# A two-block transformer kernel on one core: bias tile from 16 row copies, stacked narrow projections, last chunk by token tile, and the order of the splits

## The reference, cut to what matters

```python
# block 1
proj = rmsnorm(x) @ w_in            # qa, ka, va, qb, kb, vb, g_low (16 wide), ob, gate_a, gate_b
ya   = sliding_window_attention(qa, ka, va)  # 16 heads; score + bias[head, query - key], softmax
log_a = log_sigmoid(g_low @ w_gate_up + b_gate) / 16
ob   = gated_linear_attention(qb, kb, vb, log_a)   # 4 heads, chunks of 64 tokens
h    = x + (sigmoid(gate_a) * (ya @ w_proj_a) + sigmoid(gate_b) * (norm(ob) * silu(..) @ w_proj_b)) @ w_out
h    = h + (silu(z @ w_ffn_gate) * (z @ w_ffn_up)) @ w_ffn_down
# block 2 (input: rmsnorm(h)): memory attention over 256 memory rows, a causal convolution,
# latent attention: queries from c_q (512 wide), keys/values from c_kv (512), and one rope key
# k_rope_raw (64 wide) shared by 16 heads, rotated with cos/sin of the positions
out  = x2 + merged @ w_o            # last product of the kernel, 2048 x 2048
```

## Time and profile before

| | |
|---|---|
| median of 3 runs | 2601.61 us |
| the profiled execution's own time | 2602.74 us |
| its span | 2600.9 us |
| PE busy (matmul) | 2557.3 us, 98% |
| DVE busy | 1538.7 us, 59% |
| ACT busy | 1131.9 us, 44% |
| mean granted clock of PE | 0.995 |
| mean DMA rate | 180 GB/s |

### The profile page before, as it was taken

One profiled execution on the slowest core, in us unless ns is written; L12 is line 12 of the kernel. 1 busy time (PEld: TensorE's weight loads), 2 busy tenths in 40 slices (PEclk: granted clock), 3 DMA queues, 4 the chain that ended last, 5 costly groups with the idle time before them and its releaser, 6 DMA issues.

```text
span 2600.9 us, 30707 instructions
## 1 busy us (share of the span) xinstructions
PE 2557.3 (98%) x11746; PEld 2103.1 (81%) x11746; DVE 1538.7 (59%) x2102; ACT 1131.9 (44%) x1435; POOL 0.2 (0%) x4
## 2 busy tenths in 40 slices
PE   8899999999999999999999999999999999999999
PEld 7688777888778888888888888788888888888887
DVE  5566565466555655556556664557557757564554
ACT  4344334444444444433455454433434545444443
POOL 0000000000000000000000000000000000000000
PEclk9999999999999999999999999999999999999999
DMA  8845446655666566665656565555665455456654
GB/s 235 250 147 151 126 146 197 194 183 185 194 187 181 180 190 193 186 191 181 199 193 205 175 192 166 166 178 167 190 189 167 154 158 167 145 185 175 194 189 131
DMA packets 236404, 466.94 MB, mean 180 GB/s; under 512 B 19131, under 2 KB 27745, under 8 KB 235889
## 3 DMA queue, kind: packets, MB, share of 16 engines
q1 hardware_dynamic: 230688, 455.23, 56.4%
q10 hardware_dynamic: 5584, 9.94, 1.7%
HBM read 459.87 MB, written 5.24 MB: 179 GB/s over the span
## 4 chain that ended last, share of the span: by engine, by line
PE 90%; DVE 5%; DMA 2%; ACT 2%; issue 1%; ACTq 0%; DVEq 0%
PE acc L470 25%; PE acc L472 25%; PE acc L471 25%; PE banks L608 3%; DVE w_lo L1525 2%; PE banks L829 2%; PE banks L828 2%; PE banks L830 2%; PE acc L828 1%; PE acc L830 1%; PE acc L829 1%; DMA raw<-in_w_in_dram 1%; ACT w_hi L1119 1%; DMA arena<-bias_rows 1%; PE banks L979 1%
## 5 line engine op out<-in xcount | busy, mean ns | idle before, releaser
L1525 DVE TENSOR_TENSOR w_lo<-raw,w_hi 128x1024 fp32r<-128x1024 f32 (+1 forms) x866 | 1042.1, 1219 | 891.1 <-ACT w_hi L1119 860.4
L1119 ACT ACTIVATE w_hi<-raw 128x1024 fp32r<-128x1024 f32 (+1 forms) x866 | 904.3, 1054 | 1128.0 <-PE acc L472 1004.2
L470 PE MATMUL acc<-w_hi,x_hi_A 128*128 128x512 f32 x1880 | 746.9, 397 | 5.1 <-DVE w_lo L1525 5.1
L472 PE MATMUL acc<-w_hi,x_lo_A 128*128 128x512 f32 x1880 | 734.5, 391 | 0.0
L471 PE MATMUL acc<-w_lo,x_hi_A 128*128 128x512 f32 x1880 | 733.7, 390 | 0.0
L470 PE MATMUL acc<-w_hi,x_hi_B 128*128 128x512 f32 (+1 forms) x1216 | 474.8, 390 | 8.5 <-DVE w_lo L1525 8.5
L472 PE MATMUL acc<-w_hi,x_lo_B 128*128 128x512 f32 (+1 forms) x1216 | 471.2, 387 | 0.0
L471 PE MATMUL acc<-w_lo,x_hi_B 128*128 128x512 f32 (+1 forms) x1216 | 470.9, 387 | 0.0
L470 PEld LDWEIGHTS acc<-w_hi,x_hi_A 128*128 128x128 f32 x1880 | 354.3, 188 | 87.8 <-issue 10.2
L472 PEld LDWEIGHTS acc<-w_hi,x_lo_A 128*128 128x128 f32 x1880 | 353.9, 188 | 75.5
L471 PEld LDWEIGHTS acc<-w_lo,x_hi_A 128*128 128x128 f32 x1880 | 354.6, 189 | 71.1 <-issue 0.5
(11 more groups left out here) (263 smaller groups left out, 1336.4 us busy)
## 6 DMA issues: line engine op xcount, KB each, us to landing
raw<-in_w_in_dram SPq DMA_DIRECT2D x377, 512.0 KB, 4.4
raw<-in_w_ffn_gate_dram SPq DMA_DIRECT2D x88, 512.0 KB, 4.1
raw<-in_w_ffn_up_dram SPq DMA_DIRECT2D x88, 512.0 KB, 4.3
raw<-in_w_ffn_down_dram SPq DMA_DIRECT2D x88, 512.0 KB, 4.6
raw<-in_w_out_dram SPq DMA_DIRECT2D x32, 512.0 KB, 4.5
raw<-in_w_mem_kv_dram SPq DMA_DIRECT2D x32, 512.0 KB, 4.7
raw<-in_w_mla_out_dram SPq DMA_DIRECT2D x32, 512.0 KB, 4.7
raw<-in_w_o_dram SPq DMA_DIRECT2D x32, 512.0 KB, 4.7
```

The lines of the kernel that those rows point to most:

```text
L470: mm(o, xh, hi[:, k, :], start=(kt == first_k), stop=False)
L472: last = mm(o, xl, hi[:, k, :], start=False, stop=(kt == (last_k or c.kts) - 1))
L1119: act.activation(w_hi[:, s, 0:n], raw[:, r, 0:n], ACT.Copy).then_inc(hi_done, 1)
L1525: dve.tensor_tensor(w_lo[:, s, 0:n], raw[:, r, 0:n], w_hi32[:, s, 0:n], ALU.subtract).then_inc(lo_done, 1)
```

## The change

Seven edits go together.

1. The bias rows are written 16 times per head instead of 128 (`BCOPY`), from ScalarE's queue. The tile is read back in 8 DMAs of 16 partitions from SP's queue, after the loads of chunk `kva`, behind a wait for the write. VectorE makes the bias row ahead of the row statistics instead of in the middle of the first chunk's evacuation.
2. VectorE no longer waits for the Sin.
3. `glow` and `kr` are done with high and low weights side by side as one stationary operand (`stacked`): 32 matmuls each. `glow` leaves 32 rows, summed by a `w_gate_up` loaded twice. `kr` becomes two granules of eight k-tiles after an undivided `cq`, leaves 128 rows, and is turned and summed by two small matmuls with a folded identity before granule 4 of `ckv`.
4. The last chunk of `w_o` runs four granules as before, waits for all four others, and then does these for token tile 0 and after it for token tile 1; each tile is added and stored by itself.
5. TensorE transposes quarter 1 of `x` after granule 0, and 2 and 3 after granules 2 and 4; the split counts become 3, 2, 2, 1.
6. ScalarE does both `back(3)` of a head ahead of the Square.
7. ScalarE runs one tiny Copy before anything else, after a VectorE memset.

```diff
+BCOPY = 16
+STACKED = ("glow", "kr")
-    out += [("cq", 1, [Chunk("cq", "A", 0, CQ_HEAD, 2, CW, "w_in_2", C2["cq"])])]
-    out += [one("kr", "A", 0, KT, "w_in_2", C2["kr"], w=DR, per=16)]
-    out += [("cq_rest", 1, [Chunk("cq_rest", "A", CQ_HEAD, KT - CQ_HEAD, 2, CW, "w_in_2", C2["cq"], row=CQ_HEAD)])]
+    out += [one("cq", "A", 0, KT, "w_in_2", C2["cq"])]
+    out += [one("kr", "A", 0, KT, "w_in_2", C2["kr"], w=DR, per=8)]
...
# SP
+                if name == "kva":
+                    sp.wait_ge(b_ready, 16)
+                    for q in range(0, P, BCOPY):
+                        shifted = bass.AP(scratch.tensor, P - 1 - q, [[BIASW, BCOPY], [P * (BIASW + 1), AH], [1, 2 * P]])
+                        sp.dma_start(bias_t[q:q + BCOPY], shifted).then_inc(b_ready, 16)
...
+            for t in range(T):
+                sp.wait_ge(out_ready, 4 + t)
+                sp.dma_start(out[t * P:(t + 1) * P, 3 * CW:], xres[:, t, 3 * CW:]).then_inc(stored, 16)
...
# TensorE
+            def stacked(c):
+                w = c.w
+                o = acc[C.slot(2)][:, 0, 0:S]
+                for g in range(c.grans):
+                    pe.wait_ge(lo_done, G.at(1))
+                    both = w_hi[:, G.slot(SPL), 0:2 * c.per * w].rearrange("p (k n) -> p k n", k=c.per)
+                    for k in range(c.per):
+                        kt = g * c.per + k
+                        mm(o[0:2 * w], both[:, k, :], XH["A"][:, kt, :], start=(kt == 0), stop=False, skip_group_check=True)
+                        last = mm(o[0:w], both[:, k, 0:w], XL["A"][:, kt, :], start=False, stop=(kt == KT - 1), skip_group_check=True)
+                    last.then_inc(w_used, 1)
+                    G.n += 1
...
             turn_x(0)
-            turn_x(1)
...
-                if g in (1, 3):
-                    turn_x((g + 3) // 2)
+                if g in (0, 2, 4):
+                    turn_x(g // 2 + 1)
...
+            for g in range(c.grans):          # c is ckv
+                if g == 4:
+                    unit(rope_key)
+                    unit(turn_pair)
+                    unit(turn_pair)
+                granule(c, g, C.slot(2))
...
+            pe.wait_ge(lo_done, G.at(half))   # last chunk, after its first four granules
+            for t in range(T):
+                for g in range(half):
...
# ScalarE
+            act.wait_ge(step, 1)
+            act.activation(sm[:, 68:69], sm[:, 69:70], ACT.Copy)
...
-            for k, ahead in enumerate((1, 3, 2, 2)):
+            for k, ahead in enumerate((3, 2, 2, 1)):
...
-            copies = scratch.rearrange("h (q j) -> h q j", j=BIASW + 1)[:, :, 0:BIASW]
+            copies = bass.AP(scratch.tensor, 0, [[P * (BIASW + 1), AH], [BIASW + 1, BCOPY], [1, BIASW]])
...
-            act.wait_ge(b_ready, 16)
-            act.dma_start(bias_t, shifted).then_inc(b_ready, 16)
...
             for h in range(BH):
                 W.back(3)
+                W.back(3)
                 skip_units(3)
                 act.wait_ge(unit_done, W.U.at(1))
                 act.activation(etmp[:, 0, :], W.bank(), ACT.Square).then_inc(squares_done, 1)
                 skip_units(1)
-                W.back(3)
...
# VectorE
-            dve.wait_ge(act_done, W.R.next())
+            W.R.next()
             dve.wait_ge(mem_in, 16)
...
+            stage_normed(cgt, 1)
+            dve.wait_ge(unit_done, W.U.at(1))
             for t in range(T):
-                dve.wait_ge(unit_done, W.U.at(1))
-                TS(kr[:, t, :], W.bank()[:, 0:DR], r_two[:, t:t + 1], None, ALU.mult).then_inc(unit_free, 1)
-                dve.wait_ge(unit_free, W.U.next())
-            stage_normed(cgt)
+                ins = TS(kr[:, t, :], W.bank()[:, t * DR:(t + 1) * DR], r_two[:, t:t + 1], None, ALU.mult)
+            ins.then_inc(unit_free, 1)
+            dve.wait_ge(unit_free, W.U.next())
             W.more()
...
+            for t in range(T):
+                dve.wait_ge(part_done, 2 + t)
+                v = xres[:, t, 3 * CW:]
+                STT(v, a[:, t, :], 0.5, v, ALU.mult, ALU.add).then_inc(out_ready, 1)
```

More of the change, by code:

```diff
@@ L474, in granule @@
                 G.n += 1
[L476 to L488, removed]
@@ L939, in with_pair, with rope_key @@
                 C.n += 1
-            head = find("cq")
-            find("kr")
-            queries_and_rope_key(head, find("cq_rest"))
-            with_pair("ckv", 4)
+            one("cq")
+            one("kr")
+            def rope_key(bk, s):
+                for t in range(T):
+                    last = mm(bk[:, t * DR:(t + 1) * DR], kr_two[:, t * P:(t + 1) * P], fold, start=True, stop=True)
+                return last
+            c = find("ckv")
+            need(pe, acc_free[C.slot(2)], C.rounds(2))
+            for g in range(c.grans):
[4 more added lines that the diff above has]
+                granule(c, g, C.slot(2))
+            C.n += 1
             for h in range(2):
@@ L1013, in _ @@
             product_and_turn("mla_out", merged2, "w_o")
-            for _ in range(3):
+            for _ in range(2):
                 one("w_o")
+            c = next_one("w_o")
+            half = c.grans // 2
+            need(pe, acc_free[C.slot(2)], C.rounds(2))
+            for g in range(half):
+                granule(c, g, C.slot(2))
+            pe.wait_ge(lo_done, G.at(half))
+            for t in range(T):
+                for g in range(half):
+                    hi, lo = (w[:, G.slot(SPL, g), :].rearrange("p (k n) -> p k n", k=c.per) for w in (w_hi, w_lo))
+                    for k in range(c.per):
+                        kt = (half + g) * c.per + k
+                        xh, xl = XH[c.x][:, kt, t * P:(t + 1) * P], XL[c.x][:, kt, t * P:(t + 1) * P]
+                        o = acc[C.slot(2)][:, t, :]
+                        mm(o, xh, hi[:, k, :], start=False, stop=False)
+                        mm(o, xh, lo[:, k, :], start=False, stop=False)
+                        last = mm(o, xl, hi[:, k, :], start=False, stop=(kt == KT - 1))
+                last.then_inc(part_done, 1)
         class Walk:
@@ L1263, in _ @@
             act.wait_ge(act_req, W.R.at(1))
-            act.dma_start(w_up[0:RANK, :], ap["w_gate_up"]).then_inc(gla_in, 16)
+            for k in range(2):
+                act.dma_start(w_up[k * RANK:(k + 1) * RANK, :], ap["w_gate_up"]).then_inc(gla_in, 16)
             act.dma_start(b_gate, ap["b_gate"].rearrange("(a n) -> a n", a=1).to_broadcast([P, BH * BK])).then_inc(gla_in, 16)
```

157 lines of the change are left out of this document (61 added, 96 removed).

## The result

The changed kernel takes 2584.63 us, the median of four runs (2583.31 to 2586.96), beside 2601.97 for the kernel before in the same session (four runs, 2601.32 to 2603.15). The ratio is 0.9934, with a 95% interval of 0.9917 to 0.9951: 17.3 us faster, and the interval excludes no change. The forecast was 2584.5.

A forecast was written before the change was run, and what follows sets the result against it. TensorE was taken as the bound, 90% of the chain that ended last. The terms summed to -17.2 us, 2585.5 in the profiled execution's terms, 2584.4 against the median; forecast 2584.5 us, range 2577 to 2593, at 80%.

The forecast's parts named there:

- 1 bias tile: First attention scores: smaller bias write ends TensorE's wait and stalls on late weights; 11.6 us gained, bounds 8 to 12.7.
- 2 Sin: Memory rows: their DMA, not the Sin, ends VectorE's idle time, so dropping the wait gains 0; bounds 0 and 0.3.
- 3a glow: glow: matmuls 1.8 us shorter, following gap grows from 1.24 to 3.0; gain 0, bounds 1.8 gained or 1.2 lost.
- 3b rope key: kr and ckv: stacked kr gains 7.15 us, VectorE's new wait gives 2.2 back; net 4.9 gained, bounds 3.0 and 7.0.
- 4 last chunk: Last chunk: 2.67 us wait for low parts, smaller end saves 0.5 and 0.7; 1.5 lost, bounds 0.8 and 4.5 lost.
- 5, 7 start: Start: table load leaves the path, quarter 1 turned inside the run, slower clock; 1.2 us lost, bounds 0.5 gained, 2.6 lost.
- 6 gated heads: Four gated heads: splits ahead of the Square remove stalls before transposes; 3.4 us gained, bounds 1.5 and 4.0.
- The cover: Bias reads: weights of the 25th granule land 10 us before TensorE needs them at about 85.
- 17.6 us as before: Bias tile: the eight reads take as long as the old single read and land by 70.
- the bound of 4.5: Last chunk: worst case of 4.5 us lost, with the idle stretch halving the clock for some 6 us.
- the terms 0.88 + 0.7 + 0.2: Start: 0.88 us for eight transposes inside the run, 0.7 for more slow matmuls, 0.2 for waits on later parts.
- the term of 0.55: Start: without the table load in the path, the first granule starts 0.55 us earlier.

The follow-up runs named there:

- e1: Kernel before plus the bias edit alone (16 copies, eight reads of 16 partitions, bias row made earlier): 2590.58 us, -12.0 against the kernel before.
- e11: Changed kernel with the memory rows loaded early and VectorE's wait for the Sin put back: 2576.72 us, ratio 0.9902 to the kernel before.
- e6: Changed kernel with the load of the memory rows issued earlier, without the wait for the Sin: 2577.49 us, 7.4 faster than the changed kernel.
- e7: Changed kernel with glow as 48 matmuls again and one copy of w_gate_up, kr still stacked: 2583.99 us, 0.9 faster than the changed kernel.
- e12: Changed kernel with the rope key as in the kernel before, glow still stacked: 2590.45 us, 5.7 slower than the changed kernel.
- e2: Changed kernel with its last chunk, last scale-and-add and last store as in the kernel before: 2582.72 us, 2.6 faster than the changed kernel.
- e3: Changed kernel with quarter 2 of x turned before the first granule and the old split order, early table load kept: 2583.71 us, 1.6 faster than the changed kernel.
- e4: Changed kernel with ScalarE's old order in the gated heads, Square ahead of the second splits: 2590.16 us, 5.3 slower than the changed kernel.
- e5: Changed kernel with VectorE's low parts for ckv's granules 4 and 5 made before its rope-key wait: 2583.48 us, 1.4 faster than the changed kernel.
- e10: Changed kernel with 32 copies of each bias row instead of 16, four reads of 32 partitions: 2586.71 us, -15.4 against the kernel before.

## Why the prediction was right, and where it was off

The mechanisms were right in the main. Missed was what the clock does behind two waits, that after glow and that in the last chunk. Each term of the sum, with what the runs showed (negative is faster):

| step | predicted | by the traces | by the medians |
|---|---|---|---|
| 1 bias tile | -11.6 | -11.4 (e1); -12.5 from the end of the first chunk | -12.0 (e1) |
| 2 Sin | 0 | 0 (e11 against e6) | within 0.8 |
| 3a glow | 0 | +1.3 (e7), +2.7 with the clock's phase | +0.9 |
| 3b rope key | -4.9 | -5.2 (e12) | -5.7 |
| 4 last chunk | +1.5 | +2.7 after against before, +3.5 after against e2 | +2.6 (e2) |
| 5, 7 start | +1.2 | +1.2 (table -0.56, order +1.8); +0.8 in after's profile, whose first transfer landed 0.46 earlier | order alone +1.6 (e3) |
| 6 gated heads | -3.4 | -4.0 (e4) | -5.3 |

- **Bias.** The steps held: the write was no longer in the way (5.6 us where I took 4), TensorE was then late by VectorE's copy of the keys, 1.23 us, and the clock stayed up behind it (2.8, predicted 2.6). The cover was overrated: 6.4 us were left where I had 10. "17.6 us as before" held, since the packets of the reads lie between 55.8 and 73.6, 17.8 us, but not for the reason given: before's read ran beside weights, at 347 GB/s and more in all, these ran almost alone, at 132. What was off is the start. I had 52; the first read was issued at 53.4 and its packets began at 55.8, behind weights that were queued already.
- **Sin.** Right, for the reason given: the releaser in the earlier trace rows is the DMA.
- **glow.** "TensorE then waits for VectorE's copies" was right, 3.05 us for 3.0. "Gain 0" wasn't: the loss that I had put at the bound, an earlier fall of the clock, is what happens in most executions. A gap that grows isn't free although no work is late.
- **Rope key.** Right in both halves. 32 matmuls took 3.7 us, the new wait cost 1.02 at granule 4, and e5 shows that the wait was avoidable: it takes that 1.02 and 0.5 more away.
- **Last chunk.** The wait was 2.62 for 2.67. The smaller end saved 1.7 against before and 0.9 against e2, for 1.2. What was missing from the middle of the estimate is the clock: eight matmuls at 0.43 us, 0.2 more than at full rate, and some smaller delays, 1.8 us (2.6 + 1.8 - 1.7 is the 2.7 of the table). It stood in the bound of 4.5 and not in the value.
- **Start.** The order costs 1.8, as the terms 0.88 + 0.7 + 0.2 say. The table load gives 0.56, as the term of 0.55 says. The excess over 1.2 that after's profile shows at the end of the first chunk (38.39 against 36.65) is the profile of before: three slow matmuls there, nine in e1 with the same start.
- **Gated heads.** 4.0 for 3.4. I counted the stalls at the transposes (1.7 and 1.6) and only part of the small ones inside the heads' granules, 0.1 to 0.2 us each, which vanish as well.

By the traces the gains were 0.7 us larger than the terms (0.3 and 0.6, less 0.2 for the bias tile) and the losses 2.1 larger (1.3 and 1.2, less the 0.4 of the early first transfer). The sum of the third column, with the terms of after's own profile (+0.8, +2.7) and +1.3 for glow, is -15.8, the difference of the two profiled executions. That it fits so well is itself in part chance: the 1.4 us lost behind glow that e7 doesn't give back stand against 1.0 gained between 401 and 904 us that no term has. The medians are 17.3 apart. That the forecast met them within 0.2 us is therefore partly luck, of about 1.5 us.

## What to carry to other kernels

Price a wait that you add or lengthen twice: its own length, and what the clock may do behind it; where no work was late but a gap grew from 1.2 to 3 us, nine profiles of ten lost 1.3 us. Where a chain of two waits ends in a gap, look at the later one and move its start: issuing the load earlier was worth 7.4 us, the Sin nothing, and the space for an earlier load was free. A loop by token tile at the end needs only as many granules in it as are ready anyway: with two the end came 0.9 us earlier than with none by the traces, with four 2.6 later by the medians. Before pricing an edit at the start of a kernel, measure from the first instruction that a transfer releases, since that transfer's landing moved by up to 1.2 us from profile to profile.

## What the hardware showed that was not expected

- The same wait doesn't always bring the clock down. TensorE's wait of 2.62 us in the last chunk stands in nine profiles to within 0.01 us (after, e3 to e7, e10 to e12). Two of them (e5, e11) have no slow matmul behind it, two (e6, e12) have six from the first one on, and five have seven or eight, beginning 1.0 to 1.6 us after TensorE resumed. In after TensorE ran five matmuls at full rate, then eight at 0.43 us.
- At the start the same program differs by as much: with the old order of the start 3, 9, 9 and 4 slow matmuls in four profiles, with the new one 6 to 12 in ten. That is 0.2 us for each. With the landing of the first transfer it puts the first scores of these ten anywhere from 93.9 to 95.9 us, and the last chunk adds 0 to 1.8; this can account for much of the scatter of the changed kernel, but its runs without a profile can't be read for it. One profile is thus a poor base for any term that contains the clock.
- Transfers into 16 partitions at a time ran at 107 to 165 GB/s, and almost no weights moved beside them for 15 us; into 32 at 177 to 230 GB/s, with packets of the same 1 KB.
- The same last store of 512 KB landed after 3.6 us in before and e1 and after 2.7 in e2.
